# Pads behind the slots of w_hi and w_lo that shift their start addresses

## What is computed

```python
def expert_block(args):
    idx, e = args                       # 128 rows of one expert
    xb = xpad[idx]
    gu = xb @ w_gate_up[e] + b_gate_up[e]
    x_glu = jnp.minimum(gu[:, ::2], SWIGLU_LIMIT)
    x_lin = jnp.clip(gu[:, 1::2], -SWIGLU_LIMIT, SWIGLU_LIMIT)
    act = x_glu * jax.nn.sigmoid(SWIGLU_ALPHA * x_glu) * (x_lin + 1.0)
    return act @ w_down[e] + b_down[e]
```

## Time and profile before

| | us |
|---|---|
| median of 2 executions | 2802.78 |
| the two | 2799.86 and 2805.69 |
| the profiled execution, its own time | 2804.02 |
| its span, first to last instruction | 2802.2 |
| TensorE busy in the span | 2689.9 |
| VectorE busy | 2057.7 |
| ScalarE busy | 1626.4 |

### The profile page before, as it was taken

The page is one execution under the profiler, slowest core; times in us unless marked ns, Lnnn a source line. Parts: engine busy times, 40 slices in busy tenths (PEclk is TensorE's granted clock), DMA queues, the critical chain, the costliest instruction groups (busy, mean ns, idle before and its releaser), DMA issues.

```text
span 2802.2 us, 38484 instructions
## 1 busy us (share of the span) xinstructions
PE 2689.9 (96%) x12282; PEld 2157.9 (77%) x12282; DVE 2057.7 (73%) x2438; ACT 1626.4 (58%) x2055; POOL 243.4 (9%) x213
## 2 busy tenths in 40 slices
PE   8996999999999999999999999889999899989999
PEld 5754888888888888888878877777788787867787
DVE  4655999999999999999965567765555545877554
ACT  2322888888888888888844434534344344345443
POOL 0002111111111111111100000000000000200000
PEclk9997999999999999999999999999999999999999
DMA  8745999999999999999956654254466456534554
GB/s 319 252 148 192 354 361 362 360 359 356 369 360 363 361 356 363 363 355 359 361 195 193 192 178 153 98 172 149 146 192 223 129 188 206 157 118 136 168 187 147
DMA packets 263482, 700.34 MB, mean 250 GB/s; under 512 B 29512, under 2 KB 128240, under 8 KB 213680
## 3 DMA queue, kind: packets, MB, share of 16 engines
q1 hardware_dynamic: 249780, 685.19, 69.2%
q0 software_dynamic: 9504, 8.42, 0.9%
q10 hardware_dynamic: 4124, 5.77, 0.6%
HBM read 706.57 MB, written 23.63 MB: 261 GB/s over the span
## 4 chain that ended last, share of the span: by engine, by line
PE 84%; DVE 7%; issue 3%; DMA 3%; ACT 2%; SPq 1%; POOL 1%; POOLq 0%; DVEq 0%; ACTq 0%
PE bank L664 22%; PE bank L666 22%; PE bank L665 22%; PE bank L1173 3%; PE bank L1175 3%; PE bank L1174 3%; PE bank L790 1%; PE bank L814 1%; DMA raw<-in_w_in 1%; PE bank L1046 1%; PE bank L1012 1%; PE bank L1072 1%; PE bank L838 1%; PE bank L738 1%; DVE w_lo L1317 1%
## 5 line engine op out<-in xcount | busy, mean ns | idle before, releaser
L664 PE MATMUL bank<-w_hi,HTh 128*128 128x512 f32 x2824 | 1124.4, 398 | 17.6 <-DVE HTl L1368 9.5
L666 PE MATMUL bank<-w_hi,HTl 128*128 128x512 f32 x2824 | 1102.8, 391 | 0.0
L665 PE MATMUL bank<-w_lo,HTh 128*128 128x512 f32 x2824 | 1102.4, 390 | 0.0
L1317 DVE TENSOR_TENSOR w_lo<-raw,w_hi 128x1024 fp32r<-128x1024 f32 (+3 forms) x406 | 482.2, 1214 | 258.3 <-ACT w_hi L2293 254.0
L2293 ACT ACTIVATE w_hi<-raw 128x1024 fp32r<-128x1024 f32 (+3 forms) x406 | 421.3, 1055 | 418.9 <-PE bank L666 267.1
L664 PEld LDWEIGHTS bank<-w_hi,HTh 128*128 128x128 f32 x2824 | 532.9, 189 | 139.0 <-DVE HTl L1368 13.9
L666 PEld LDWEIGHTS bank<-w_hi,HTl 128*128 128x128 f32 x2824 | 532.6, 189 | 114.5
L665 PEld LDWEIGHTS bank<-w_lo,HTh 128*128 128x128 f32 x2824 | 533.4, 189 | 103.0
L1964 DVE TENSOR_TENSOR w_lo<-arena,w_hi 128x1024 fp32r<-128x1024 f32 x256 | 316.1, 1235 | 38.6 <-ACT w_hi L2491 22.3
L1964 DVE TENSOR_TENSOR w_lo<-raw,w_hi 128x1024 fp32r<-128x1024 f32 x256 | 298.9, 1220 | 3.6 <-ACT w_hi L2536 3.6
L2491 ACT ACTIVATE w_hi<-raw 128x1024 fp32r<-128x1024 f32 x252 | 268.0, 1063 | 55.6 <-PE bank L666 55.6
(11 more groups left out here) (365 smaller groups left out, 2707.9 us busy)
## 6 DMA issues: line engine op xcount, KB each, us to landing
raw<-in_moe_w SPq DMA_DIRECT2D x128, 1024.0 KB, 6.8
arena<-in_moe_w SPq DMA_DIRECT2D x128, 1024.0 KB, 6.6
H<-in_moe_w SPq DMA_DIRECT2D x64, 1024.0 KB
MIX<-in_moe_w SPq DMA_DIRECT2D x64, 1024.0 KB
raw<-in_ffn_w SPq DMA_DIRECT2D x248, 256.0 KB, 3.4
raw<-in_ffn_w_gu SPq DMA_DIRECT2D x164, 256.0 KB, 3.4
raw<-in_w_in SPq DMA_DIRECT2D x76, 512.0 KB, 4.8
raw<-in_ffn_w_down SPq DMA_DIRECT2D x80, 256.0 KB, 3.3
```

What stands on the lines that cost most here:

```text
L664: pe.matmul(acc, xh, wh, start=start, stop=False)
L665: pe.matmul(acc, xh, wl, start=False, stop=False)
L666: return pe.matmul(acc, xl, wh, start=False, stop=stop)
L1317: dve.tensor_tensor(lo_at(n, c), raw_at(n, c), hi_at(n, c).bitcast(F32), ALU.subtract).then_inc(lo_done, 1)
```

## The change

A slot of w_hi and w_lo gets 1026 elements in place of 1024; the last two (8 bytes) are never used. A tensor pad_between of 4 bytes stands between w_hi and w_lo, and one of 188 bytes, pad_behind, behind w_lo. Tensors are placed one behind another, each at the next multiple of 32 bytes. So w_hi stays at 146080, w_lo moves from 162464 to 162528, and the tensors from BIAS on move by 288 bytes, BIAS from 178848 to 179136. The slots start at 32, 40, 48 and 56 modulo 64 in w_hi and in w_lo. The instructions that fill a slot name its first 1024 elements; no instruction is added, removed or moved.

```diff
--- before.py
+++ after.py
@@ -164,8 +164,10 @@
         EXTRA += [arena_r[:, a:a + 2 * TILE] for a in IN_ARENA]
         EXTRA_RAW = [t[:, :, :].rearrange("p a b -> p (a b)") for t in (QT, KT, Y, MIX, H)]
         EXTRA_RAW += [arena[:, a:a + 2 * TILE] for a in IN_ARENA]
-        w_hi = sb("w_hi", [P, PARTS, TILE], F32R)
-        w_lo = sb("w_lo", [P, PARTS, TILE], F32R)
+        w_hi = sb("w_hi", [P, PARTS, TILE + 2], F32R)
+        sb("pad_between", [P, 1])
+        w_lo = sb("w_lo", [P, PARTS, TILE + 2], F32R)
+        sb("pad_behind", [P, 47])
         BIASR = sb("BIAS", [P, 8, S], F32R)
         BIAS = BIASR[:, :, :].bitcast(F32)
         VEC = sb("VEC", [P, VECS, D])
@@ -1961,7 +1963,7 @@
             def lows(it, first, last):
                 for t in range(first, last):
                     dve.wait_ge(m_hi, it * MOE_TILES + t + 1)
-                    dve.tensor_tensor(w_lo[:, t % PARTS, :], moe_raw(t), w_hi[:, t % PARTS, :].bitcast(F32),
+                    dve.tensor_tensor(w_lo[:, t % PARTS, 0:TILE], moe_raw(t), w_hi[:, t % PARTS, 0:TILE].bitcast(F32),
                                       ALU.subtract).then_inc(m_lo, 1)
 
             def take_linear(it, half):
@@ -2488,7 +2490,7 @@
                 for t in range(first, last):
                     act.wait_ge(m_landed[t // 2 % MOE_SLOTS], it * (16 * MOE_TILES // (2 * MOE_SLOTS)) + 16 * (t // (2 * MOE_SLOTS) + 1))
                     act.wait_ge(m_used, moe_used(it, t - PARTS))
-                    act.activation(w_hi[:, t % PARTS, :], moe_raw(t), ACT.Copy).then_inc(m_hi, 1)
+                    act.activation(w_hi[:, t % PARTS, 0:TILE], moe_raw(t), ACT.Copy).then_inc(m_hi, 1)
 
             def take_glu(it, half):
 
@@ -2533,7 +2535,7 @@
             act.wait_ge(tile_used, moe_at)
             for t in range(PARTS):
                 act.wait_ge(m_landed[t // 2], 16)
-                act.activation(w_hi[:, t, :], moe_raw(t), ACT.Copy).then_inc(m_hi, 1)
+                act.activation(w_hi[:, t, 0:TILE], moe_raw(t), ACT.Copy).then_inc(m_hi, 1)
             high_of(7, 0, XETh, 1, m_gather, m_xhi)
             high_of(7, 1, XETh, 2, m_gather, m_xhi)
             with act.Fori(0, last) as it:
```

## The result

The changed kernel takes 2842.18 us (two executions, 2841.82 and 2842.53) against 2802.78, 39 us more; the ratio on record is 1.0136 with a 95% interval of 1.0115 to 1.0157. The forecast was 2828 in a range of 2780 to 2862, slower by under 2%. The size of its one term was too small; where it looked was right.

A forecast was written before the change was run, and what follows sets the result against it. TensorE was taken to bound the kernel: 9,432 matmuls times the distance between their starts. Only those matmuls got a cost, 25 us, the other terms 0: 2804 + 25 = 2829, or 2828 against the median; range 2780 to 2862.

The forecast's parts named there:

- (a): ACT's copies into w_hi and DVE's subtractions into w_lo: pace unchanged, 0 us.
- (b): The 4 x 32 matmuls with BIAS and SELB, which move together, and the fp32 transposes by TAB: 0 us.
- (c): The 9,432 matmuls reading w_hi or w_lo: mean start distance from 228 to 230.6 ns, +2.6 each, 25 us.
- slot 0 was to recover: Matmuls of slot 0, still at residue 32: 230 ns for six after entry, 228.4 for twelve, taken as 229.
- 324-column rows: Products reading w_hi at residues 32, 48 and 0 at 148.6 ns a start; taken as evidence of nothing lost, weighted one third.
- 512-column rows: Arena tiles off their stationary operand's residue, at 233.3 ns a start against 226.7; weighted two thirds for slots 1 to 3.
- Residue modulo 64: Moving operand's start against its stationary operand's, modulo 64 bytes, sets the matmul pace; differing ones lose about 7 ns.
- No effect: Rival: residues do not change the matmul pace, steady 226.7 ns, 2803 us within 10; chance 0.27.
- its account of the arena tiles by region: Rival's claim that arena tiles at 233.3 ns are slow for the region they lie in, not their residue.
- Much slower through starts at 8 modulo 16: Rival: slots 1 and 3 stumble more than any row shows, +113 us, 2916; slower by over 2% had chance 0.10.
- the 240 ns that was this rival's sign: Start distances above 240 ns in slots 1 and 3 would prove the much slower case.
- The faster ones: Rivals: new residues shorten matmul starts, -42 us (2761) or, at fp32's 214.4 ns, -128 us (2675); chances 0.13 and 0.06.

The follow-up runs named there:

- e1_behind: Against the kernel before: slots unmoved, only the tensors behind w_lo moved by 288 bytes; 2803.93 us, ratio 1.0004.
- e9_padsonly: Against the kernel before: the change's slot pads (stride 4104), with w_lo's start and all behind moved by whole multiples of 256 bytes; 2842.61 us, ratio 1.0119.
- e7_off64: Against the kernel before: all slots and all behind moved by 64 bytes, stride 4096; 2817.35 us, ratio 1.0057.
- e11_off128: Against the kernel before: all slots and all behind moved by 128 bytes; 2845.79 us, ratio 1.0133.
- e3_off8: Against the kernel before: all slots moved by 8 bytes, stride 4096, and w_lo by 64 more; 2845.85 us, ratio 1.015.
- e8_off256: Against the kernel before: all slots and all behind moved by 256 bytes, stride 4096; 2801.8 us, ratio 1.0007.
- e10_lo64: Against the kernel before: no slot pads, w_lo alone starts 64 bytes later, all behind moved by 256; 2837.17 us, ratio 1.0104.
- e6_stat32: Against the kernel before: stationary operands HTh, HTl, AFTh, AFTl moved by 32 bytes, w_hi, w_lo and all behind by 512; 2844.79 us, ratio 1.0152.
- e5_both32: Against the kernel before: stationary operands, w_hi, w_lo and all behind moved together by 32 bytes; 2805.67 us, ratio 1.001.

## Why the prediction was right, and where it was off

**What bounds the kernel.** Right: the start distances, times 9,432, give 38.2 us where the spans differ by 37.8. The count is a little off, since 96 of the 9,432 have 324 or 160 columns and not 512, which is 1% of the term.

**Terms (a) and (b).** ACT and DVE kept their lengths, and all that lies behind the slots can move for 1.0004 (e1_behind). The reason given for (b) was incomplete: BIAS and SELB keep their relation to each other, but the timeline has each weight load beside the matmul ahead of its own, so BIAS streams while a piece of HTh is loaded, and those two now stand 32 bytes apart modulo 256. In e1_behind that touches 128 matmuls and their neighbours: where nothing breaks in, the distance behind a bias matmul goes from 226.7 to 230.0 ns, and in sum it isn't measurable.

**Term (c).** This is the term that was mis-sized: +2.6 ns were forecast, +4.05 measured, 25 us against 38. Two of its steps failed. First, slot 0 was to recover. For the slot pads alone that was sound: in e9_padsonly it takes 230.7 ns in the experts' stage, where 230 was put, and in the first product 229.0 and then 226.7 for its two sixes. But in the changed kernel w_lo's slot 0 is at offset 64 while w_hi's is at 0, and there is no recovery: 231.0 and 232.9 ns for the two sixes in the first product, where 228.4 stood for the twelve. Second, the 324-column rows were weighted in for "nothing lost", a third. They couldn't tell: in e7_off64 and e11_off128, where all their pieces lie at other offsets than before, they take 148.2 and 149.5 ns against 148.6, and 150.6 in the slowest kernel (e3_off8), so at that width offsets cost 2 ns at most, while at 512 columns every offset under 256 bytes that was tried costs more than that. The slots at 8, 16 and 24 bytes have 235.4, 231.9 and 233.4 ns (e9_padsonly) and not 231.1. With the 233.3 of the 512-column rows unweighted, the same sum gives (229 + 3 x 233.3) / 4 = 232.2, and 9,432 x 4.2 = 40 us.

**The address rule.** "Residue modulo 64" was read off rows in which all fast tiles agree modulo 256 too: HTh 84640, w_hi 146080, w_lo 162464 and QT 105120 are all 160 modulo 256, the arena's start is 128 and IN_A5 144. I saw a difference of 32 and of 16 bytes and took the nearest round number for the width. e7_off64, e8_off256 and e11_off128 show that it is 256. So w_lo's move from 162464 to 162528, which the prediction counted as none, is one of 64 bytes, and by e10_lo64 it costs 1.0% alone. The forecast doesn't owe its direction to this: e9_padsonly, which has only what the prediction counted, costs 1.0119.

**The rivals.** No effect: it fell, as did its account of the arena tiles by region (e6_stat32). Much slower through starts at 8 modulo 16: fell, since e6_stat32 has none and is as slow as the change; in e9_padsonly slots 1 and 3, which have them, take 235.4 and 233.4 ns and slot 2, which has not, 231.9, on average all under the 240 ns that was this rival's sign, though single steps of slot 1 reach 243. The faster ones: no offset tried beats 0, and the fp32 pace of 214.4 ns was nowhere reached as a mean. The Trainium skill ("TensorE: Matmul & The Clock Gate", Part 2, step by step) states that loading the next weights takes no read bandwidth from the running matmul. These fp32r matmuls don't bear that out: e6_stat32 moves only the operand that the weight load reads, and the starts go from 226.7 to 233.3 ns apart.

What stays open: what the two reads meet in, why the good distance is 226.7 and not 214.4, and the price of the offsets that weren't tried, a steady 32 among them. Between 128 and 256 the record has two values besides 224 (233.3 ns, e6_stat32): IN_A5, at 240, has 233.3 ns in the earlier trace rows, and 18 arena tiles of e5_both32, at 192 since HTh had moved, also 233.3.

## What to carry to other kernels

For full-rate fp32r matmuls of 512 columns like these, keep the moving and the stationary operand at the same address modulo 256 bytes, in every tensor and every slot; a pad of a few bytes, or a tensor put between them, can cost over 1% of a kernel that TensorE bounds. When a change of layout is judged, read the start distances in a stretch without waits: 200 of them gave 226.7 ns in all four kernels at offset 0, while executions of the kernel before lay between 2797.26 and 2812.3 us. And print the addresses of the built program, of the experiments too: here 4 bytes became 32, and a helper that rounds up moved w_lo by 64 bytes more in two runs that were meant to move it by 8 and 32.

## What the runs showed of the hardware that was not expected

That the pace of the moving stream depends at all on where the weight load of the same engine reads, by 2 to 9 ns of 227 at the offsets tried, and with a period of 256 bytes in the distance. And that it is gone at the lower clock. In the changed kernel's first product, three starts after TensorE had waited for 2.4 us, comes a stretch at 1.2 GHz. From its timeline, and the clock of that stretch from the busy times by window (the third column from the end):

```profile
42.65 0.50 PE L666 MATMUL bank<-w_hi,HTh 128*128 128x512 f32 x1 [2.40 <-DVE HTl L1370]
```

```profile
43.91:46.47 2.56, 2.56 (x7) 1.94 (x6) 2.56 (x3) 0.00 (x0) 0.00 (x0) 0.50 0.53 118
```

```profile
43.91 0.63 PE L667 MATMUL bank<-w_lo,HTh 128*128 128x512 f32 x1
...
46.47 0.56 PE L667 MATMUL bank<-w_lo,HTh 128*128 128x512 f32 x1
```

46.47 - 43.91 = 2.56 us for six, 426.7 ns each, which is 512 / 1.2 to the digit: no loss, with w_hi at offset 0 and w_lo at 64. At 2.4 GHz the same pair of offsets loses 19 ns over 213.3 (e10_lo64, 232.1). It is so at the steady offset of e6_stat32 too: eleven distances from 43.10 us on take 4.69 us at a granted clock of 0.50, 426.7 ns each. So in these stretches the columns come without a stall, at half the pace.
